# A hybrid Hyena, attention and expert layer: fewer transfers for attention's values, a merge that begins with the attention branch, and two banks for the first expert's tokens

## The chip, the cores and the metric

The kernel runs on one core of one Trainium2 chip. The metric is the device time of one execution in microseconds; a time is the median of several executions. The engines are TensorE (PE, with PEld for its weight loads), VectorE (DVE), ScalarE (ACT), GpSimd (POOL) and SyncE (SP). SP and POOL issue nearly all the transfers.

## What is computed

One layer over 1024 latent tokens (a grid of 16 rows by 64 columns) and 256 context tokens, width 1024, everything in float32:

```python
hx = modulate(rmsnorm(x), sh1, sc1); zx = hx @ w_in + b_in      # one combined projection
hy_x = hyena_mixer(zx[..., :COL_Q], ...)                        # two long convolutions
na_x = na_latent(q, k, v, kc, vc, rpb)                          # neighbourhood attention, 8 heads
a = hy_x @ w_branch_hy;  b = na_x @ w_branch_na                 # the merge
mix = (sigmoid(g_hy) * a + sigmoid(g_na) * b) @ w_out
x = x + g1 * mix
h = modulate(rmsnorm(x), sh2, sc2)
aff = softmax(h @ w_router); g, idx = top_k(aff.T, 128)         # 16 experts choose 128 tokens each
y_e = (silu(h[idx] @ wg) * (h[idx] @ wu)) @ wd                  # per expert
x = x + g2 * scatter_add(g_e * y_e);  out = rmsnorm(x) * final_g
```

Attention for a query uses keys and values in a window of 8 rows by 16 columns, and all 256 context tokens.

## The kernel before

The work is a row of blocks, one after the other: projection, attention (`attend`), Hyena (`hyena`), `merge`, `project_out`, `choose`, `experts`. In a block each engine has its own program and they wait for one another by semaphores; no engine begins the next block before all have ended this one. Each float32 product is made of three products of parts: an operand is split by ACT into a rounded high part (`*_hi`), by DVE into the rest (`*_lo = raw - hi`), and TensorE multiplies hi by hi, hi by lo and lo by hi.

**Values.** The last part of the projection computes the values, tile by tile of 128 tokens: TensorE fills a bank, DVE adds the bias into `v_stage` (L841), POOL stores the tile to `v_d` in DRAM (L392). Attention wants them laid out in `v_band`: a block holds four grid rows by a box of 32 columns, on 128 partitions. `load_values(sp, a, keep, kg)` loads, for the four grid rows of `kg`, four boxes `b`, in four transfers each, one for each grid row `r`. SP issues those of `kg` 0 to 2 at the end of the projection block, behind the stores of the normed tokens' parts to `hq_d` (L351), each `kg` behind a wait for two tiles stored (`stored`); then it waits for `kept`, and the block may end. Those of `kg` 3 it issues first in the attention block, behind the last tiles' stores; behind them come the tables and the heads (`load_table`, `load_head`). The first product of attention's probabilities and values waits for `v_in[0]` (`kg` 0 to 2), the fifth for `v_in[1]`. TensorE's steps in attention are: scores of step s, transposes of step s-2, product of step s-3.

**End of Hyena.** Hyena has four passes (p from 0 to 3) and the gates' projection (`gates(n)`, 32 of them, products L1399) is spread between them by the table `SHARE`. In the last pass DVE makes `products` and `transform` (L1512 to L1552), then raises `y_ready`; TensorE makes `outputs(3, i)` for i from 0 to 3 (L1382) and DVE `gated(3, i)` (L1564, L1572), which end the block with `y_t`. ACT's last works are the gates' sigmoids (L1454); SP stores each (L1275).

**Merge.** SP loads the first slices of the branch weights (`b_raw`), then attention's output `na_d` into `na_t`, then weights and gates (`g_d`). ACT and DVE split `y_t` (4 quarters), the weights' slice 0, then `na_t` (4 quarters). TensorE multiplies for output slice d=0: Hyena's branch for both token halves, then attention's; each branch of a half is 12 matmuls of 512 columns. DVE gates and adds. The loop over d from 1 to 7 follows.

**Experts.** The weights come in units of 1 MB (`raw`, 8 slots, 33 units for each expert, 528 in all); ACT splits a unit (L2251), DVE makes its low part (L2303), TensorE uses it in 12 matmuls (L2210 gate and up, L2200 down). Units 0 and 1 are the gate's of chunk 0 (unit 0 uses the tokens' rows k 0 to 3, unit 1 k 4 to 7), 2 and 3 the up's, 4 to 7 those of chunk 1. ACT and DVE take work in one written order:

```python
for g in range(N_ALL + N_U):
    if AHEAD <= g < N_ALL:
        split(g)
    for e, what, c in steps(g):
```

By that order DVE's `multiply` of chunk 0 (`moe_h`, L2324) stands behind `split(9)`, and ACT's `silu` behind `split(7)`. `split(g)` for g of 6 and more waits until unit g-6 is used. After unit 5 TensorE transposes this `h` (`turn_h(0, 0)`, L2181) and then goes to unit 6. At the start POOL gathers the first expert's tokens `xe`; TensorE transposes them in two halves (`turn_x`, L2173, four transposes each) in one bank `ps_x`; ACT copies the high part (L2244), DVE the low part (L2294). The second half's transposes wait for the first half's low part, and unit 0 waits for both. DVE makes the splits 0 to 2, three small works and only then the low parts.

Of the kernel before, what the change touches and what calls it, by code (L numbers as in the profile page):

```python
# [9 lines left out]
F32 = mybir.dt.float32  # L10
# [6 lines left out]
P = 128  # L17
# [865 lines left out]
def attend(nc, sems, a, keep):  # L883
# [3 lines left out]
    with ExitStack() as ctx:  # L887
# [55 lines left out]
        with nc.Block() as block:  # L943
# [23 lines left out]
            def _(pe):  # L967
# [206 lines left out]
def hyena(nc, sems, a, keep, y_t):  # L1174

    par, ident = keep["par"], keep["ident"]
    with ExitStack() as ctx:
# [25 lines left out]
        decay_in, gate_in, v2_in = keep["w_mod_in"][0:3]  # L1203
        LOADED = 16 * MOD_CHUNKS
# [48 lines left out]
        with nc.Block() as block:  # L1253

            @block.sync
            def _(sp):
# [178 lines left out]
            def _(act):  # L1435
# [20 lines left out]

                for p in range(-1, PASSES):
# [17 lines left out]
                    for n in AT_END[p]:  # L1475
                        gates(n)

            @block.vector
            def _(dve):
# [107 lines left out]
                for p in range(PASSES):  # L1587
                    q = p + 1
                    coming = iter(range(PH if q < PASSES else 0))

                    def decay_next():
                        for r in itertools.islice(coming, 1):
# [5 lines left out]
                    for r in coming:  # L1598
# [10 lines left out]

def merge(nc, sems, a, keep, y_t, m_t):  # L1610

    with ExitStack() as ctx:
        m = Maker(nc, ctx, "merge_")
        in_hi, in_lo = m.sb("in_hi", [P, 2, 4, T], F32R), m.sb("in_lo", [P, 2, 4, T], F32R)
        na_t = m.sb("na_t", [P, 4, T])
        b_raw = m.sb("b_raw", [P, 2, 2, 4, P])
        b_hi, b_lo = m.sb("b_hi", [P, 2, 2, 4, P], F32R), m.sb("b_lo", [P, 2, 2, 4, P], F32R)
        gate = m.sb("gate", [P, 2, 2, T])
        ps = m.psum("ps", [P, 4, 2, 512])


        w_in = [sems(f"branch_in{s}") for s in range(2)]
        g_in = [sems(f"gates_in{s}") for s in range(2)]
        na_in = sems("na_in")
        in_hi_ready, in_lo_ready, bh_ready, bl_ready, branched, merged = (
            sems(n) for n in ("in_hi_ready", "in_lo_ready", "bh_ready", "bl_ready", "branched", "merged"))

        with nc.Block() as block:

            @block.sync  # L1630
            def _(sp):
                w = [a[n].rearrange("(k p) (d c) -> d p k c", p=P, c=P) for n in ("w_branch_hy", "w_branch_na")]
                g = a["g_d"].rearrange("(b d p) t -> b d p t", b=2, p=P)
                wo = a["w_out"].rearrange("(k p) n -> p k n", p=P)
                for b in range(2):
                    sp.dma_start(b_raw[:, 0, b], w[b][0]).then_inc(w_in[0], 16)
                for k in range(4):
                    sp.dma_start(na_t[:, k], a["na_d"][k]).then_inc(na_in, 16)
# [14 lines left out]
            def _(pe):  # L1653
                pe.sem_inc(branched, 4)

                def branch(s, th, b, first=False):
                    for k in range(4):
                        if first:
                            pe.wait_ge(in_lo_ready, 4 * b + k + 1)
                        hi, lo = b_hi[:, s, b, k, :], b_lo[:, s, b, k, :]  # L1660
                        cols = slice(th * 512, (th + 1) * 512)
                        for x, (w, h) in enumerate(((hi, in_hi), (hi, in_lo), (lo, in_hi))):
                            mm = pe.matmul(ps[:, 2 * s + th, b, :], w, h[:, b, k, cols],
# [17 lines left out]
            def _(act):  # L1681
# [5 lines left out]
                for b, src in enumerate((y_t, na_t)):  # L1687
                    if b:
                        split(0, 0, 0)
                        act.wait_ge(na_in, 64)  # L1690
                    for k in range(4):
# [813 lines left out]
```

## Time and profile before

| | |
|---|---|
| median of three runs | 2703.47 us (2702.67 to 2703.78) |
| the profiled execution's own time | 2703.3 us |
| its span, first to last instruction | 2700.7 us |
| PE busy | 2545.6 us, 94% |
| DVE busy | 2121.3 us, 79% |
| ACT busy | 1469.9 us, 54% |
| mean granted TensorE clock | 0.973 |
| bytes moved | 794.93 MB, mean 294 GB/s |

The profile is one execution. A share of busy time is a mean over stages; what a stage is worth is read from its own stretch. The time outside the span is 2.6 us.

### The profile page before, as it was taken

How to read it: one execution, taken by the hardware profiler on the slowest of the kernel's cores; microseconds unless marked ns; L12 is line 12 of the kernel's file. 1: busy time of each engine (PE TensorE's matmuls, PEld its weight loads, DVE VectorE, ACT ScalarE, POOL GpSimd, SP SyncE). 2: the span in 40 equal slices, each digit the busy share in tenths (PEclk: the TensorE clock that was granted, in tenths of full speed). 3: DMA queues.
4: the chain of work that ended last, by engine and by line, in shares of the span. 5: the costliest groups of instructions: out<-in, count | busy, mean ns of one | idle time of the engine just before them, and what ended most of it. 6: DMA issues, size and time to landing. Idle time of an engine off the chain costs nothing.

```text
span 2700.7 us, 32209 instructions
## 1 busy us (share of the span) xinstructions
PE 2545.6 (94%) x12577; PEld 2121.3 (79%) x12577; DVE 2121.3 (79%) x1976; ACT 1469.9 (54%) x1249; POOL 149.3 (6%) x159
## 2 busy tenths in 40 slices
PE   6999979999999899389999999999999999999997
PEld 2777869878878778368888888888888888888885
DVE  5674247667879555688888888889888888888887
ACT  4522136531121222177777777777777777777774
POOL 0011000011111000000000000000000000000000
PEclk9999989999999999689999999999999999999998
DMA  7498774464566733399999999999999999999994
GB/s 272 161 314 306 248 228 111 135 200 140 162 200 197 236 104 131 155 339 362 386 390 373 374 392 381 363 383 394 370 373 392 380 366 383 389 375 367 392 382 171
DMA packets 198628, 794.93 MB, mean 294 GB/s; under 512 B 17935, under 2 KB 65399, under 8 KB 128528
## 3 DMA queue, kind: packets, MB, share of 16 engines
q1 hardware_dynamic: 168196, 704.75, 69.4%
q0 software_dynamic: 30128, 88.11, 10.6%
q8 instruction: 98, 1.61, 0.2%
q14 instruction: 48, 0.39, 0.0%
q10 hardware_dynamic: 158, 0.07, 0.0%
HBM read 723.38 MB, written 69.48 MB: 294 GB/s over the span
## 4 chain that ended last, share of the span: by engine, by line
PE 53%; ACT 2%; issue 2%; DVE 1%; DVEq 0%; ACTq 0%
PE moe_ps_gate L2210 18%; PE moe_ps_up L2210 16%; PE moe_ps_y L2200 16%; PE moe_ps_h L2181 2%; ACT moe_w_hi L2251 1%; PE moe_ps_x L2173 1%; DVE raw L2373 0%; ACT moe_xt_hi L2244 0%; DVE moe_w_lo L2303 0%; DVE moe_h L2324 0%; ACT moe_sl L2264 0%; DVE raw L2360 0%; PE moe_ps_gate L2234 0%; PE moe_ps_gate L2236 0%; PE moe_ps_up L2234 0%
## 5 line engine op out<-in xcount | busy, mean ns | idle before, releaser
L2303 DVE TENSOR_TENSOR moe_w_lo<-raw,moe_w_hi 128x2048 fp32r<-128x2048 f32 x528 | 1207.6, 2290 | 159.8 <-ACT moe_w_hi L2251 159.6
L2251 ACT ACTIVATE moe_w_hi<-raw 128x2048 fp32r<-128x2048 f32 x528 | 1011.0, 1919 | 379.2 <-PE moe_ps_gate L2210 128.4
L2210 PE MATMUL moe_ps_up<-moe_w_hi,moe_xt_hi 128*128 128x512 f32 (+1 forms) x768 | 292.4, 381 | 0.0
L2210 PE MATMUL moe_ps_gate<-moe_w_hi,moe_xt_hi 128*128 128x512 f32 (+1 forms) x768 | 289.1, 376 | 1.4 <-DVE moe_xt_lo L2294 1.4
L2210 PE MATMUL moe_ps_gate<-moe_w_hi,moe_xt_lo 128*128 128x512 f32 (+1 forms) x768 | 286.5, 373 | 0.0
L2210 PE MATMUL moe_ps_up<-moe_w_hi,moe_xt_lo 128*128 128x512 f32 (+1 forms) x768 | 286.4, 373 | 0.0
L2210 PE MATMUL moe_ps_gate<-moe_w_lo,moe_xt_hi 128*128 128x512 f32 (+1 forms) x768 | 286.1, 373 | 0.0
L2210 PE MATMUL moe_ps_up<-moe_w_lo,moe_xt_hi 128*128 128x512 f32 (+1 forms) x768 | 285.9, 372 | 0.0
L2200 PE MATMUL moe_ps_y<-moe_w_hi,moe_ht_hi 128*128 128x512 f32 x704 | 218.5, 392 | 0.0
L2200 PE MATMUL moe_ps_y<-moe_w_hi,moe_ht_lo 128*128 128x512 f32 x704 | 217.0, 389 | 0.0
L2200 PE MATMUL moe_ps_y<-moe_w_lo,moe_ht_hi 128*128 128x512 f32 x704 | 217.0, 389 | 0.0
L1399 PE MATMUL hyena_ps_g<-hyena_h_parts,hyena_g_parts 128*128 128x512 f32 x768 | 182.5, 395 | 2.0 <-DMA hyena_h_parts<-hq_d 1.9
L1399 PEld LDWEIGHTS hyena_ps_g<-hyena_h_parts,hyena_g_parts 128*128 128x128 f32 x768 | 144.0, 188 | 33.3 <-issue 1.9
L2210 PEld LDWEIGHTS moe_ps_gate<-moe_w_hi,moe_xt_hi 128*128 128x128 f32 x768 | 145.2, 189 | 26.4 <-DVE moe_xt_lo L2294 1.8
L2210 PEld LDWEIGHTS moe_ps_gate<-moe_w_hi,moe_xt_lo 128*128 128x128 f32 x768 | 145.1, 189 | 25.6
L2210 PEld LDWEIGHTS moe_ps_gate<-moe_w_lo,moe_xt_hi 128*128 128x128 f32 x768 | 145.3, 189 | 24.8
L2210 PEld LDWEIGHTS moe_ps_up<-moe_w_hi,moe_xt_lo 128*128 128x128 f32 x768 | 144.5, 188 | 25.6
L2210 PEld LDWEIGHTS moe_ps_up<-moe_w_lo,moe_xt_hi 128*128 128x128 f32 x768 | 144.8, 189 | 23.7
L2210 PEld LDWEIGHTS moe_ps_up<-moe_w_hi,moe_xt_hi 128*128 128x128 f32 x768 | 144.7, 188 | 23.3
L2200 PEld LDWEIGHTS moe_ps_y<-moe_w_lo,moe_ht_hi 128*128 128x128 f32 x704 | 132.2, 188 | 27.8
L2200 PEld LDWEIGHTS moe_ps_y<-moe_w_hi,moe_ht_lo 128*128 128x128 f32 x704 | 132.2, 188 | 27.7
L1512 DVE TENSOR_TENSOR hyena_spec<-hyena_spec 128x1024 f32<-128x1024 f32 (+2 forms) x120 | 139.4, 1217 | 16.1 <-ACT hyena_spec L1447 15.8
(278 smaller groups left out, 3707.1 us busy)
## 6 DMA issues: line engine op xcount, KB each, us to landing
raw<-in_w_moe SPq DMA_DIRECT2D x528, 1024.0 KB, 7.2
hyena_g_parts<-gw_d POOLq DMA_DIRECT2D x64, 512.0 KB, 4.7
proj_w_mod<-in_w_mod SPq DMA_DIRECT2D x32, 512.0 KB, 7.3
gw_d<-proj_g_parts POOLq DMA_DIRECT2D x16, 1024.0 KB, 7.4
w_in<-in_w_in SPq DMA_DIRECT2D x12, 1024.0 KB, 7.6
attn_table<-in_na_table SPq DMA_DIRECT2D x16, 576.0 KB, 5.6
norm_w_mod<-in_w_mod SPq DMA_DIRECT2D x16, 512.0 KB, 7.1
proj_g_raw<-in_w_in SPq DMA_DIRECT2D x16, 512.0 KB, 9.5
```

The costliest lines, as they stand in the source:

```text
L1399: mm = pe.matmul(ps_g[:, n % 2, :], g_parts[:, g % G_SLOTS, w, k % G_K, :], h_parts[:, h, k, :], start=(k == 0 and y == 0), stop=(k == KD ...
L1512: dt.inc(dve.tensor_tensor(out, in0, in1, op))
L2173: mm = pe.transpose(ps_x[:, k * P:(k + 1) * P], xe[:, at:at + P], ident[:])
L2181: mm = pe.transpose(ps_h[:, b * P:(b + 1) * P], h[:, c % 2, b * P:(b + 1) * P], ident[:])
L2200: mm = pe.matmul(ps_y[:, n * 512:(n + 1) * 512], hp, wp[:, r, n * 512:(n + 1) * 512], start=(first and x == 0), stop=(last and x == 2))
L2210: mm = pe.matmul(ps, hp[:, e % 2, k, :], wp[:, r, :], start=(k == 0 and x == 0), stop=(k == KD - 1 and x == 2))
L2251: act.activation(w_hi[:, g % PARTS], raw[:, g % RAW], ACT.Copy).then_inc(hi_ready, 1)
L2303: dve.tensor_tensor(w_lo[:, g % PARTS], raw[:, g % RAW], w_hi[:, g % PARTS].bitcast(F32), ALU.subtract).then_inc(lo_ready, 1)
```

## The change

Three parts. (A) `load_values` issues one transfer for each box instead of one for each box and grid row: its source has three dimensions (4 grid rows, 32 columns, 512 numbers of 4 bytes), its target all 128 partitions. The counts waited for shrink to match. (B) The merge's tiles are placed before Hyena; SP, ACT and DVE load and split slice 0 of the branch weights and the first quarter of attention's output inside Hyena's last pass (`na_raw` has three slots; the fourth quarter is loaded once the first is split), ACT makes the high parts of the other quarters at the end of the Hyena block, DVE their low parts first in the merge block; TensorE takes attention's branch first. (C) In the expert block, 36 transposes of the identity stand ahead of the first `turn_x`; the second half of expert 0 goes to the bank `ps_h`; unit 0 waits for the first half only, unit 1 for the second; DVE makes the two low parts after split 1.

```diff
-def load_values(sp, a, keep, kg):
+def load_values(eng, a, keep, kg):
     for b in range(4):
-        for r in range(4):
-            first = (4 * kg + r) * GRID_W + BAND_AT[b]
-            sp.dma_start(keep["v_band"][BAND * r:BAND * (r + 1), v_block(kg, b), 0:HEADS * HD],
-                         a["v_d"][first:first + BAND]).then_inc(keep["v_in"][kg // 3], 16)
+        first = 4 * kg * GRID_W + BAND_AT[b]
+        rows = bass.AP(a["v_d"].tensor, first * HEADS * HD, [[GRID_W * HEADS * HD, 4], [HEADS * HD, BAND], [1, HEADS * HD]])
+        eng.dma_start(keep["v_band"][:, v_block(kg, b), 0:HEADS * HD], rows).then_inc(keep["v_in"][kg // 3], 16)
...
-                        pe.wait_ge(v_in[g], 16 * 48 if g == 0 else 16 * 16)
+                        pe.wait_ge(v_in[g], 16 * 12 if g == 0 else 16 * 4)
...
+                def load_na(k):
+                    s = k % NA_SLOTS
+                    if k >= NA_SLOTS:
+                        sp.wait_ge(na_lo_ready, k - NA_SLOTS + 1)
+                    sp.dma_start(coming["na_raw"][:, s], a["na_d"][k]).then_inc(na_in, 16)
...
+                        if p == PASSES - 1 and r == 1:
+                            sp.wait_ge(tap_used, PH * PASSES)
+                            sp.wait_ge(a_done, a_at["seg", p, PH - 1] + 1)
+                            for b, w in enumerate(branch_sources(a)):
+                                sp.dma_start(coming["b_raw"][:, 0, b], w[0]).then_inc(branch_in[0], 16)
+                            for k in range(NA_SLOTS):
+                                load_na(k)
...
+                load_na(NA_SLOTS)
                 sp.wait_ge(g_kept, 16 * N_G)
...
+                    if p == PASSES - 1:
+                        act.wait_ge(branch_in[0], 32)
+                        act.activation(coming["b_hi"][:, 0], coming["b_raw"][:, 0], ACT.Copy).then_inc(bh_ready, 1)
+                        act.wait_ge(out_done, NB * p)
+                        high_na(0)
...
+                for k in range(1, 4):
+                    high_na(k)
...
                     dve.sem_inc(y_ready, 1)
-                    for r in coming:
+                    if p == PASSES - 1:
+                        dve.wait_ge(bh_ready, 1)
+                        dve.tensor_tensor(coming["b_lo"][:, 0], coming["b_raw"][:, 0], coming["b_hi"][:, 0].bitcast(F32),
+                                          ALU.subtract).then_inc(bl_ready, 1)
+                        low_na(dve, coming, 0)
+                    for r in decays_left:
...
+def low_na(dve, at, k):
+    dve.wait_ge(at["in_hi_ready"], k + 1)
+    dve.tensor_tensor(at["lo"][1][:, k], at["na_raw"][:, k % NA_SLOTS], at["hi"][1][:, k].bitcast(F32), ALU.subtract
+                      ).then_inc(at["in_lo_ready"], 1)
...
                 pe.wait_ge(bl_ready, 3)
-                branch(0, 0, 0, first=True)
-                branch(0, 1, 0)
+                branch(0, 0, 1, first=True)
+                branch(0, 1, 1)
                 for th in range(2):
-                    branch(0, th, 1, first=not th).then_inc(branched, 1)
+                    branch(0, th, 0, first=not th).then_inc(branched, 1)
...
+                for k in range(1, 4):
+                    low_na(dve, at, k)
+                for k in range(4):
+                    dve.wait_ge(in_hi_ready, 4 + k + 1)
+                    dve.tensor_tensor(in_lo[0][:, k, :], y_t[:, k, :], in_hi[0][:, k, :].bitcast(F32),
+                                      ALU.subtract).then_inc(in_lo_ready, 1)
...
+        WARM = 36
...
+        def x_turned(e, half):
+
+            return ps_h if (e, half) == (0, 1) else ps_x
...
+                for n in range(WARM):
+                    pe.transpose(ps_x[:, n % 4 * P:(n % 4 + 1) * P], ident[:], ident[:])
                 turn_x(0, 0)
                 turn_x(0, 1)
                 for e in range(E_N):
-                    pe.wait_ge(x_parts, 2 * e + 2)
+                    if e:
+                        pe.wait_ge(x_parts, 2 * e + 2)
                     for u in range(N_U):
+                        if e == 0 and u < 2:
+                            pe.wait_ge(x_parts, u + 1)
...
-                for g in range(AHEAD):
+                split(0)
+                split(1)
+                for half in range(2):
+                    low_x(0, half)
+                for g in range(2, AHEAD):
                     split(g)
```

## Rows read from the trace of the kernel before

**Rows 1.** The chain that ended last, in order of time: start, duration, what

```profile
1182.76 5.51 PE moe_ps_up L2210 x24
...
1276.95 5.49 PE moe_ps_up L2210 x24
```

**Rows 2.** Timeline, 355 to 400 us: start, duration, engine, line, what, [idle before, releaser]

```profile
360.09 0.54 POOL L392 DMA_DIRECT2D v_d<-attn_v_stage  x1 [4.95 <-DVE attn_v_stage L841]
...
373.26 0.66 PE L990 MATMUL attn_ps_s<-attn_k_hi,attn_q_two 128*128 128x384 f32 x1 [14.20 <-PEq L266]
...
381.92 1.82 PE L1022 MATMUL attn_ps_o<-v_band,attn_prob_t 128*128 128x128 f32 x10
```

**Rows 3.** Timeline of SP's queue, 325 to 400 us, then 370 to 374 us

```profile
332.89 3.78 SPq L351 DMA_DIRECT2D hq_d<-h_lo  x1
336.78 43.62 SPq L163 DMA_DIRECT2D v_band<-v_d  x64
...
369.87 4.50 SPq L163 DMA_DIRECT2D v_band<-v_d  x9
```

**Rows 4.** Lines 163, 392, 351 (landing), 1275: issue ns min/median/max, landing

```profile
L163 SPq DMA_DIRECT2D v_band<-v_d x64: 312/422/8769, 336.8 to 380.0; - x64
DMA to landing us min/median/max: 1.8/1.9/15.1
...
DMA to landing us min/median/max: 2.7/5.8/8.9
...
DMA to landing us min/median/max: 18.5/22.2/24.5
...
L1275 SPq DMA_DIRECT2D g_d<-hyena_g_out x6: 319/320/320, 849.8 to 876.6; - x6
```

**Rows 5.** Timeline of all engines, 856 to 912 us

```profile
877.39 7.77 PE L1382 MATMUL hyena_ps_out<-idft,hyena_spec 128*128 128x128 f32 x64 [1.74 <-DVEq L1597]
879.48 0.87 DVE L1564 SCALAR_TENSOR_TENSOR y_t<-y_t,par,hyena_ps_out 128x256 f32<-128x256 f32 x2 [2.20 <-PE hyena_ps_out L1382]
...
886.16 0.76 DVE L1572 TENSOR_TENSOR y_t<-y_t,hyena_gate 128x256 f32<-128x256 f32 x2
...
887.22 3.90 ACT L1692 ACTIVATE merge_in_hi<-y_t 128x1024 fp32r<-128x1024 f32 x4 [10.68 <-PEq L1253]
...
888.31 4.63 DVE L1726 TENSOR_TENSOR merge_in_lo<-y_t,merge_in_hi 128x1024 fp32r<-128x1024 f32 x4 [1.39 <-ACT merge_in_hi L1692]
...
892.86 1.22 DVE L1705 TENSOR_TENSOR merge_b_lo<-merge_b_raw,merge_b_hi 128x1024 fp32r<-128x1024 f32 x1
...
894.13 0.79 PE L1663 MATMUL merge_ps<-merge_in_hi,merge_b_hi 128*128 128x512 f32 x1 [8.97 <-DVE merge_b_lo L1705]
...
907.46 1.29 DVE L1716 TENSOR_TENSOR merge_gate<-merge_ps,merge_gate 128x512 f32<-128x512 f32 x2 [0.47 <-PE merge_ps L1663]
```

**Rows 6.** Windows: us; busy PE, PEld, DVE, ACT, POOL; clock, DMA share, GB/s

```profile
373.00:383.00 10.00, 8.11 (x32) 7.58 (x33) 8.03 (x14) 6.81 (x9) 0.00 (x0) 0.50 0.51 134
...
1163.00:1168.00 5.00, 4.92 (x12) 3.86 (x13) 3.82 (x3) 4.70 (x3) 0.00 (x0) 0.50 0.80 298
```

**Rows 7.** Timeline of all engines, 1143 to 1186 us

```profile
1152.41 6.70 DVE L2303 TENSOR_TENSOR moe_w_lo<-raw,moe_w_hi 128x2048 fp32r<-128x2048 f32 x3 [2.22 <-ACT moe_w_hi L2251]
...
1156.48 1.12 PE L2173 MATMUL moe_ps_x<-identity,moe_xe 128*128 128x128 f32 x4 [7.33 <-DMA moe_xe<-h_d,idx_col]
1157.63 0.60 ACT L2244 ACTIVATE moe_xt_hi<-moe_ps_x 128x512 fp32r<-128x512 f32 x1 [1.66 <-PE moe_ps_x L2173]
...
1159.80 0.69 DVE L2294 TENSOR_TENSOR moe_xt_lo<-moe_ps_x,moe_xt_hi 128x512 fp32r<-128x512 f32 x1 [0.21 <-DVE moe_chosen L2312]
...
1163.08 0.80 PE L2210 MATMUL moe_ps_gate<-moe_w_hi,moe_xt_hi 128*128 128x512 f32 x1 [1.41 <-DVE moe_xt_lo L2294]
...
1164.20 11.33 DVE L2303 TENSOR_TENSOR moe_w_lo<-raw,moe_w_hi 128x2048 fp32r<-128x2048 f32 x5 [1.18 <-ACT moe_w_hi L2251]
...
1181.36 0.68 DVE L2324 TENSOR_TENSOR moe_h<-moe_sl,moe_ps_up 128x512 f32<-128x512 f32 x1
```

More of the change, by code:

```diff
@@ L1203, in hyena @@
         decay_in, gate_in, v2_in = keep["w_mod_in"][0:3]
+        coming = keep["merge"]
+        branch_in, na_in, na_hi_ready, na_lo_ready, bh_ready, bl_ready = (
+            coming[n] for n in ("w_in", "na_in", "in_hi_ready", "in_lo_ready", "bh_ready", "bl_ready"))
         LOADED = 16 * MOD_CHUNKS
@@ L1607, in _, with merge_places, branch_sources @@
                         transform(U_LEAF[q], U_SPEC[q], nothing)
+NA_SLOTS = 3
+def merge_places(nc, sems):
+    with ExitStack() as ctx:
+        m = Maker(nc, ctx, "merge_")
+        at = {"b_raw": m.sb("b_raw", [P, 2, 2, 4, P]),
+              "b_hi": m.sb("b_hi", [P, 2, 2, 4, P], F32R), "b_lo": m.sb("b_lo", [P, 2, 2, 4, P], F32R)}
+        m.sb("room", [P, PH * 2 * P])
+        at["na_raw"] = m.sb("na_raw", [P, NA_SLOTS, T])
+        hi, lo = [None, None], [None, None]
+        hi[0], hi[1] = m.sb("y_hi", [P, 4, T], F32R), m.sb("na_hi", [P, 4, T], F32R)
+        at["gate"] = m.sb("gate", [P, 2, 2, T])
+        lo[0], lo[1] = m.sb("y_lo", [P, 4, T], F32R), m.sb("na_lo", [P, 4, T], F32R)
+        at["hi"], at["lo"] = hi, lo
+    at["w_in"] = [sems(f"branch_in{s}") for s in range(2)]
+    for n in ("na_in", "in_hi_ready", "in_lo_ready", "bh_ready", "bl_ready"):
+        at[n] = sems(n)
+    return at
+def low_na(dve, at, k):
+    dve.wait_ge(at["in_hi_ready"], k + 1)
+    dve.tensor_tensor(at["lo"][1][:, k], at["na_raw"][:, k % NA_SLOTS], at["hi"][1][:, k].bitcast(F32), ALU.subtract
+                      ).then_inc(at["in_lo_ready"], 1)
+def branch_sources(a):
+    return [a[n].rearrange("(k p) (d c) -> d p k c", p=P, c=P) for n in ("w_branch_hy", "w_branch_na")]
 def merge(nc, sems, a, keep, y_t, m_t):
@@ L1613, in merge @@
         m = Maker(nc, ctx, "merge_")
[L1614 to L1618, printed above, removed]
+        at = keep["merge"]
+        b_raw, b_hi, b_lo, gate, in_hi, in_lo = (at[n] for n in ("b_raw", "b_hi", "b_lo", "gate", "hi", "lo"))
         ps = m.psum("ps", [P, 4, 2, 512])
-        w_in = [sems(f"branch_in{s}") for s in range(2)]
+        w_in, in_hi_ready, in_lo_ready, bh_ready, bl_ready = (
+            at[n] for n in ("w_in", "in_hi_ready", "in_lo_ready", "bh_ready", "bl_ready"))
         g_in = [sems(f"gates_in{s}") for s in range(2)]
-        na_in = sems("na_in")
-        in_hi_ready, in_lo_ready, bh_ready, bl_ready, branched, merged = (
-            sems(n) for n in ("in_hi_ready", "in_lo_ready", "bh_ready", "bl_ready", "branched", "merged"))
+        branched, merged = (sems(n) for n in ("branched", "merged"))
         with nc.Block() as block:
@@ L1685, in split @@
                     act.activation(b_hi[:, s], b_raw[:, s], ACT.Copy).then_inc(bh_ready, 1)
[L1687 to L1691, printed above, removed]
-                        act.activation(in_hi[:, b, k, :], src[:, k, :], ACT.Copy).then_inc(in_hi_ready, 1)
+                for k in range(4):
+                    act.activation(in_hi[0][:, k, :], y_t[:, k, :], ACT.Copy).then_inc(in_hi_ready, 1)
                 with act.Fori(0, KD // 2 - 1) as i:
@@ L2166, in turn_x @@
                 def turn_x(e, half):
-                    if half or e:
+                    if e:
                         pe.wait_ge(x_parts, 2 * e + half)
@@ L2172, in turn_x @@
                         at = (4 * half + k) * P
-                        mm = pe.transpose(ps_x[:, k * P:(k + 1) * P], xe[:, at:at + P], ident[:])
+                        mm = pe.transpose(x_turned(e, half)[:, k * P:(k + 1) * P], xe[:, at:at + P], ident[:])
                     mm.then_inc(turned_x, 1)
@@ L2254, in _ @@
                     split(g)
-                high_x(0, 0)
-                high_x(0, 1)
+                for half in range(2):
+                    high_x(0, half)
                 for g in range(N_ALL + N_U):
@@ L2304, in split @@
                                       ALU.subtract).then_inc(lo_ready, 1)
-                for g in range(AHEAD):
+                split(0)
+                split(1)
+                for half in range(2):
+                    low_x(0, half)
+                for g in range(2, AHEAD):
                     split(g)
@@ L2417, in program @@
                 y_t = Maker(nc, mixer).sb("y_t", [P, 4, T])
+                keep["merge"] = merge_places(nc, sems)
                 n = Maker(nc, convolving)
```

35 lines of the change are left out of this document (15 added, 20 removed).

## The prediction, made before the changed kernel was seen

> **What bounds the kernel now.** I read the chain that ended last first. From unit 6 of the first expert on it is TensorE alone: the same matmuls of the up part come 94.19 us apart [rows 1], and so on to the last expert. So nothing of this change lasts beyond the first expert, and what moves unit 6 moves the end by as much. Ahead of the experts the blocks follow one another with a meeting of all engines between them, so a block that ends sooner brings everything forward. I then looked, with the timeline, for TensorE's long idle times ahead of unit 6 in the places that the diff touches. There are three: 14.20 us before attention's first matmul [rows 2], 8.97 us before the merge's first [rows 5], and the wait before the first expert's first matmul, which begins at 1163.08 though the tokens had come by 1156.48 [rows 7]. The clock column of the windows says what they also cost: granted 0.50 (1.2 GHz) in the first 10 us of attention and in the first 5 us of the experts [rows 6].
>
> **Part A, attention's values.** TensorE and DVE are done with the projection by 359.8, and POOL's last work in it, the issue of the last value tile's store, ends at 360.09 + 0.54 = 360.63 [rows 2]. ACT has long been idle. What ends the block is SP: nine issues take 4.50 us, 0.50 each, and the 64 of them end at 380.40 [rows 3]. Sixteen belong to the next block, so the 48th ended about 16 x 0.46 = 7.4 us sooner, at 373.0, and attention starts at 373.1 to 373.3 [rows 2]. The change leaves 12 issues in this block. What does one of four times the size take? From below, 0.32 us: the store of the gates' bank is also 256 KB, 128 rows of 2 KB [rows 4]. From above, four times the small one, 4 x 0.46 = 1.8 us, if the issue goes by rows. I take 0.5, near the row with the same shape. The first issue is held up for 8.77 us behind the four stores to `hq_d`, of which the last was issued at 332.89 [rows 3] and lands 22.2 us later in the median, at 355 [rows 4]. Even if the first group of four boxes is held until then, the other 8 issues take 4 us: 359. The third group also waits for a tile whose store is two tiles of 5.49 us ahead of the last, at 349.1 [rows 2], and lands 5.8 us later (at most 8.9): 355 to 358, and 4 issues more, 357 to 360. The wait for `kept` is over by about 355. So SP ends at 357 to 360, before POOL's 360.63; the meeting costs about 0.3 (886.92 to 887.20 at the end of Hyena [rows 5]), and attention starts at 360.9 instead of 373.2: 12.3 us gained. What is late next? The first product needs the three groups' data; it stood 8.7 us after the block's start [rows 2], which gives 369.6, and the last of those transfers, issued by 360, has until then (landing 1.9 in the median for the small ones [rows 4]). The fourth group waits for the last tile's store, 360.6 + 5.8 = 366.4, then 4 x 0.5 and its landing: about 372, against the fifth product at about 379. The tables and heads behind it on SP's queue come 9 us or more earlier than before. The clock: TensorE now idles 2 us instead of 14, but its first ten microseconds are filled only 8.11 of 10 at the low clock [rows 6] and DVE has its own long works there; between nothing and 1.5 us more; I take 0.4. Part A: -12.7.
>
> **Part B, the merge.** Inside Hyena it adds, on SP, two transfers of 256 KB and three of 512 KB behind the second of the six gate stores of this stretch (849.8 to 876.6, so 5.4 us apart in the mean [rows 4]). At 0.5 us an issue [rows 3] they take 2.5 us, less than the distance to the next store. Their two waits are for Hyena's tap and segment work of the pass before, over by then. Their 2 MB compete with the gates' weights; TensorE waits 1.74 us at the end of this pass for DVE [rows 5], which covers that much delay, and I charge nothing. ACT gets two copies of about 1 us (its quarters cost 3.90 / 4) ahead of its last sigmoid, which ended 10.68 us before 887.22, at 876.5 [rows 5]; nobody but its own store waits for it, which has 10 us: covered. DVE gets 1.22 + 1.16 us behind `y_ready` (quarters cost 4.63 / 4) and had 2.20 us idle there [rows 5]: 0.2 to 0.4 late, I take +0.3. At the end SP's fourth quarter is issued at 880.2, and if it lands as a value tile of half its size does at most, 5.8 us later [rows 4], ACT's copy ends at 887: about the block's own end, so the block ends at 887.2 + 0.3.
>
> In the merge, DVE needs 3 x 1.16 for attention's quarters 1 to 3 (until 891.0), then 4 x 1.16 for `y_t` (until 895.7). ACT's `y_t` copies take 3.90 [rows 5] and are ahead of it. TensorE starts at 887.6 on quarter 0. At the low clock 12 matmuls take 5 us [rows 6], at the full one 24 take 5.5 [rows 1]. If it starts low, attention's first half fills 887.8 to 892.9; with the clock up then (as at the experts' start, where it stayed low for 5 us of matmuls [rows 6]), three groups of 12 at 2.73 follow: 901.1; Hyena's last quarter at 895.7 is in time for its use after 895.7. If it stays high throughout: DVE's 891.0 + 0.7, then 2.7 three times: 899.9. Before, the 48 matmuls began at 894.13 and were done by 907.0 (DVE waits 0.47 us and gates from 907.46 [rows 5]). Gain 5.9 or 7.1, less 0.3 already in the start of the first; I take 5.9. Slice 1's weights are issued at 887.7 and are wanted as low part at 901: 13 us for a landing, a copy of 1 and a difference of 1.22 [rows 5]. Part B: -5.9, between -4.5 and -7.
>
> **Part C, the first expert.** This is the part where the obvious sum misleads. TensorE's side: tokens at 1156.48, four transposes 1.12, ACT 0.60, DVE 0.69 [rows 7]; with the new order unit 0 can start at 1156.5 + 1.15 + 0.65 + 0.7 = 1159.0 instead of 1163.08, and if the extra transposes have raised the clock, it saves the 2.3 us by which the first 12 matmuls (5.0 us [rows 6]) exceed 2.7. That reads as 4.1 + 2.3 = 6.4 us. But after unit 5 TensorE needs `h` of chunk 0, and DVE's multiply stands behind its splits 2 to 9. It ended at 1181.36 + 0.68 = 1182.04 with DVE nearly full from 1164.20 on: five splits in 11.33, 2.26 each [rows 7]. In the changed order DVE has splits 0 and 1 until 1152.41 + 4.5 = 1156.9, waits for ACT until 1158.3, then 2 x 0.69, split 2 (2.26), its small works 0.5, splits 3 to 9 (7 x 2.26 = 15.8) and the multiply 0.68: 1158.3 + 1.4 + 2.3 + 0.5 + 15.8 + 0.7 = 1179.0. ACT's splits and the units that they wait for run ahead of that. TensorE would be through unit 5 by 1159.0 + 6 x 2.72 = 1175.3 and then wait 3.7 us, a new wait in place of the old. Unit 6 gains 1182.0 - 1179.0 = 3.0 us, clock or no clock. After it DVE is again in time: splits 10 and 11 and the low part of `h` end at 1184.3, unit 8 needs them at 1185.1.
>
> The 36 transposes are no gain by this sum, only a risk: four at the low clock take 1.12 [rows 7], 0.23 each, so 36 take up to 8.3 us from the block's start, until 1158.8 (ACT's first split, of which DVE's at 1152.41 waits, puts the start at 1150.5 [rows 7]); if the clock rises after 5 us and the rest run at about half that, they end at 1157.1. The first means the tokens' transposes start 2.3 us late and DVE's row of work with them: gain 0.8. The second 0.6 late: 2.5. I take 2.5, as dense TensorE work has raised the clock within some 5 us at this place before [rows 6], and keep 0.8 as a case of its own.
>
> The Trainium skill, page "TensorE: Matmul & The Clock Gate", section "Part 4: PE-mode transpose", says that transposes in that mode do not bring on the full clock, as they don't count as TensorE activity in the same way. No row here has transposes alone for so long, so none agrees or disagrees. By it part C would be -0.8 instead of -2.5.
>
> **Sum.** -12.7 - 5.9 - 2.5 = -21.1 us. The profiled execution, 2700.7 of span and 2.6 outside it, becomes 2679.6 and 2.6, 2682.2; its 2703.3 is 0.2 under the median, so 2682.4.
>
> **The rivals.** (1) *The issue goes by rows, not by transfer*, or the 12 large ones are held up behind `hq_d` as long as the 48 were. For it: the first issue was held up for 8.77 us. Against: the 256 KB store issued in 0.32 [rows 4]. Part A gives 0 to 4 instead of 12.7: 2691 to 2695. (2) *TensorE's own sum holds in part C*: DVE's splits would have to take 1.8 us instead of 2.26, as nine works stand ahead of the multiply; against it, those five in 11.33 us [rows 7]. Part C -6.4, 2678.5. (3) *The transposes stay slow*: all 36 run at the pace of the four, end at 1158.8, 2.3 us after the tokens have come, and hold back the tokens' transposes and DVE: part C -0.8, 2684.1. (4) *Part B does nothing*, as the fourth quarter lands late or the gates' weights are delayed beyond the 1.74 us: 2688.3. (5) *Slower.* The transfers over four boxes land so late that attention stands at its first product, which waits for all 12. They are 3 MB; while the small ones moved, the core's traffic was 134 GB/s [rows 6]. The start of the first product is 369.6 if they are in time, and part A's 12.7 and the others' 8.4 would have to be lost, so the case decides once they land after 369.6 + 21.1 = 390.7; at 396, 5 us slower, 2709. That is 3 MB in 36 us from 360, under 90 GB/s; against it stand the 298 GB/s of the experts' start [rows 6].
>
> **How the numbers follow.** The forecast (2679.5 to 2686 by its own bounds): 0.44. Rival 3: 0.30. Rival 1: 0.08. Rival 2 and other larger gains, the clock in attention among them: 0.08. Rival 4: 0.05. Rival 5: 0.03. A result near no change, A, B and C all losing what they gave: 0.02. 0.2% is 5.4 us, about what a measurement of this kernel tells from no change. Faster 0.95, same 0.02, slower 0.03. The parts' bounds are A -11 to -14, B -4.5 to -7, C -0.8 to -6.4: -16.3 to -27.4 if all fell together, of which the far end is unlikely; I give 2677.5 to 2689.5, which leaves out rivals 1, 5 and the worse half of 4.
>
> **What the changed profile would show.** Attention's first matmul 2 to 3 us after the projection's last, with SP no longer last (wrong if SP's issues run past 361). The merge's first matmul within 0.7 us of the block's start, its first gating by DVE about 13 us after it. In the experts: the 36 transposes end before or after the tokens come, with the clock column at 0.5 or 1.0; unit 0 4 us earlier against the block's start; and a new wait of 2 to 4 us of `turn_h(0, 0)` for DVE's `moe_h`. If that wait is missing and unit 6 is 6 us earlier, step C is wrong. The prediction is wrong as a whole if the start of attention doesn't move.

## The result, and the profile after

The changed kernel takes 2711.96 us (median of 7 runs, 2710.43 to 2715.95) where the kernel before took 2702.75 beside it (7 runs, 2700.76 to 2703.78): a ratio of 1.0039, 95% interval 1.0030 to 1.0048. It is 9.2 us slower; 21 us faster was forecast. The profiled execution took 2712.3 us.

Read part by part, the loss lies in one place. First attention's start, in the timeline of the changed kernel, SyncE's queue and then the rows of TensorE, ScalarE and VectorE that waited. These rows answer to [rows 2, 3]:

```profile
335.53 47.61 SPq L163 DMA_DIRECT2D v_band<-v_d  x16
383.19 5.49 SPq L156 DMA_DIRECT2D attn_table<-in_na_table  x2
388.78 3.24 SPq L148 DMA_DIRECT2D attn_q_raw<-qk_d  x1
396.63 2.21 SPq L156 DMA_DIRECT2D attn_table<-in_na_table  x2
398.94 3.04 SPq L148 DMA_DIRECT2D attn_q_raw<-qk_d  x1
...
373.96 0.66 PE L989 MATMUL attn_ps_s<-attn_k_hi,attn_q_two 128*128 128x384 f32 x1 [15.95 <-PEq L265]
384.65 1.97 PE L1021 MATMUL attn_ps_o<-v_band,attn_prob_t 128*128 128x128 f32 x10 [2.21 <-DMA v_band<-v_d]
401.96 2.50 PE L1021 MATMUL attn_ps_o<-v_band,attn_prob_t 128*128 128x128 f32 x10 [6.42 <-DMA v_band<-v_d]
413.17 1.30 PE L973 MATMUL attn_ps_t<-identity,attn_prob 128*128 128x128 f32 x5 [3.52 <-ACT attn_prob_t L1054]
...
406.92 0.82 DVE L1103 CUSTOM_DVE_ANT_0 attn_score<-attn_ps_s,attn_table 128x640 f32<-128x640 f32 x1 [1.93 <-DMA attn_table<-in_na_table]
411.38 1.06 ACT L853 ACTIVATE attn_q_two<-attn_q_raw 128x1024 fp32r<-128x1024 f32 x1 [2.58 <-DMA attn_k_raw<-qk_d]
```

Sixteen issues end at 383.14, where 64 ended at 380.40 [rows 3]. Attention starts at 373.96, 16.3 us behind the projection's last matmul (357.62), where it was 14.6. Then TensorE stands twice for the values (2.21 and 6.42 us), and behind them on SyncE's queue the tables and heads are late as well: VectorE waits 1.93 us for a table, ScalarE 2.58 for a head, TensorE 3.52 for ScalarE. From its first matmul to Hyena's first matmul, attention takes 180.8 us instead of 164.7.

The duration of the 16 issues (view of one line: count, shortest/median/longest in ns, first and last start), and the windows of the changed kernel (columns as in [rows 6]):

```profile
L163 SPq DMA_DIRECT2D v_band<-v_d x16: 1780/2548/6878, 335.5 to 380.8; - x16
...
365.00:370.00 5.00, 0.00 (x0) 0.00 (x0) 0.00 (x0) 0.00 (x0) 0.00 (x0) 0.50 0.26 98
370.00:374.00 4.00, 0.04 (x1) 0.07 (x1) 0.00 (x0) 0.23 (x1) 0.00 (x0) 0.50 0.26 98
390.00:400.00 10.00, 5.54 (x47) 5.33 (x44) 4.90 (x16) 4.93 (x7) 0.00 (x0) 0.95 1.04 199
```

An issue takes 2.55 us, not 0.5. The two last columns say why to look at the transfer and not at the queue: while nothing but these transfers moves, the DMA engines are busy a steady 0.26 of the time, at 98 GB/s. That share is a mean over 16 engines, so 0.26 is what four of the sixteen give if they are at work all the time. The trace's single packets bear it out: from 365 to 373 us four packets are in flight in 84% of the instants, and never fewer. Before, the small transfers moved 144 GB/s from 365 to 370 us.

The merge and the first expert gained nearly what was forecast. Merge, VectorE's splits of attention's quarters, and the gating that answers to the one at 907.46 in [rows 5]:

```profile
905.72 0.47 PE L1719 MATMUL merge_ps<-merge_na_hi,merge_b_hi 128*128 128x512 f32 x1 [2.38 <-DVEq L1753]
905.60 3.50 DVE L1667 TENSOR_TENSOR merge_na_lo<-merge_na_raw,merge_na_hi 128x1024 fp32r<-128x1024 f32 x3 [0.50 <-PEq L1255]
919.29 1.29 DVE L1768 TENSOR_TENSOR merge_gate<-merge_ps,merge_gate 128x512 f32<-128x512 f32 x2 [0.47 <-PE merge_ps L1719]
```

The merge's block starts at 905.4, so this gating comes 13.9 us into the merge, where it was 20.3: 6.4 us gained. From Hyena's first matmul to that start it is 350.6 us instead of 349.2. Experts, TensorE and VectorE, the rows that answer to [rows 7]:

```profile
1162.56 6.25 PE L2273 MATMUL moe_ps_x<-identity 128*128 128x128 f32 x36 [1.35 <-PEq L2034]
1168.96 0.65 PE L2229 MATMUL moe_ps_x<-identity,moe_xe 128*128 128x128 f32 x4 [0.16 <-DMA moe_xe<-h_d,idx_col]
1174.55 15.51 DVE L2366 TENSOR_TENSOR moe_w_lo<-raw,moe_w_hi 128x2048 fp32r<-128x2048 f32 x7
1189.96 0.68 DVE L2389 TENSOR_TENSOR moe_h<-moe_sl,moe_ps_up 128x512 f32<-128x512 f32 x1
1190.70 1.05 PE L2239 MATMUL moe_ps_h<-identity,moe_h 128*128 128x128 f32 x4 [3.06 <-DVE moe_h L2389]
```

The new wait of `turn_h(0, 0)` for VectorE's multiply is there, 3.06 us long (3.7 forecast). It has a price that the forecast left out. The granted clock is still 1.00 while TensorE waits, and 0.50 once it works again, so the 24 matmuls of units 6 and 7 take 6.69 us where they took 5.51 before ([rows 1], 1182.76). The windows are read as in [rows 6], the last row is from the chain that ended last:

```profile
1188.00:1190.00 2.00, 0.00 (x0) 0.00 (x0) 2.00 (x2) 1.65 (x1) 0.00 (x0) 1.00 0.99 418
1191.00:1194.00 3.00, 3.00 (x10) 2.52 (x9) 3.00 (x2) 1.09 (x2) 0.00 (x0) 0.50 1.00 418
...
1191.76 6.69 PE moe_ps_up L2268 x24
```

### The profile page after: what moved, and what is told of

It reads as the page before. It is cut to its first block, busy times and chain, and to the rows that moved or that the text cites. A ratio compares the mean times of both kernels' runs of the same rounds, so it can differ in the third digit from the quotient of the medians.

```text
span 2710.6 us, 32235 instructions
## 1 busy us (share of the span) xinstructions
PE 2554.4 (94%) x12613; PEld 2129.3 (79%) x12613; DVE 2121.2 (78%) x1976; ACT 1469.6 (54%) x1249; POOL 149.1 (6%) x159
## 4 chain that ended last, share of the span: by engine, by line
PE 52%; issue 2%; ACT 2%; DVE 1%; DMA 0%; DVEq 0%; ACTq 0%; POOLq 0%
PE moe_ps_gate L2268 18%; PE moe_ps_y L2258 16%; PE moe_ps_up L2268 16%; PE moe_ps_h L2239 2%; ACT moe_w_hi L2314 1%; PE moe_ps_x L2229 1%; DVE moe_w_lo L2366 0%; DVE raw L2438 0%; ACT moe_xt_hi L2307 0%; DVE moe_h L2389 0%; ACT moe_sl L2327 0%; DMA moe_xe<-h_d,idx_col 0%; DVE raw L2425 0%; PE moe_ps_gate L2297 0%; PE moe_ps_gate L2299 0%
## 5 line engine op out<-in xcount | busy, mean ns | idle before, releaser
L2258 PEld LDWEIGHTS moe_ps_y<-moe_w_lo,moe_ht_hi 128*128 128x128 f32 x704 | 132.2, 188 | 27.8
L2258 PEld LDWEIGHTS moe_ps_y<-moe_w_hi,moe_ht_lo 128*128 128x128 f32 x704 | 132.2, 188 | 27.8
L1540 DVE TENSOR_TENSOR hyena_spec<-hyena_spec 128x1024 f32<-128x1024 f32 (+2 forms) x120 | 139.6, 1219 | 16.1 <-ACT hyena_spec L1463 15.8
```

The lines of the kernel that those rows point to most:

```text
L1540: dt.inc(dve.tensor_tensor(out, in0, in1, op))
L2258: mm = pe.matmul(ps_y[:, n * 512:(n + 1) * 512], hp, wp[:, r, n * 512:(n + 1) * 512], start=(first and x == 0), stop=(last and x == 2))
```

## The experiments

Theory 1: a transfer whose source pattern has an outermost dimension of 4 is carried by 4 of the 16 DMA engines; it is slow, holds back the issue of the next, and all that stands behind it. Theory 2: an issue costs by its rows or bytes. Theory 3: the stores of `hq_d` in front hold everything up. Each kernel is compared with the kernel before on the same chip: bc_only, rows128, by_row and two_rows with 2701.87 us (12 runs), a_only, last_stores, two_queues and no_warm with 2702.82 (11 runs), early_multiply and last_stores_again with 2701.96 (11 runs). The table gives, for the profiled execution of each kernel, how many us behind the projection's last matmul attention's first one starts, and how many us pass from there to Hyena's first matmul.

| kernel | median, us | start of attention | attention |
|---|---|---|---|
| before | 2702 to 2703 | 14.6 | 164.7 |
| after | 2711.96 | 16.3 | 180.8 |
| bc_only | 2692.77 | 13.3 | 165.0 |
| a_only | 2722.01 | 16.4 | 180.5 |
| rows128 | 2687.27 | 8.4 | 164.6 |
| by_row | 2690.95 | 10.6 | 164.6 |
| two_rows | 2753.68 (one run) | 48.0 | 192.0 |
| last_stores | 2682.28 | 3.8 | 164.5 |
| two_queues | 2683.64 | 3.3 | 164.6 |

### The parts by themselves: bc_only and a_only

bc_only leaves `load_values` and its counts as they were before; a_only changes `load_values` and its counts and nothing else.

> Parts B and C alone; the values are loaded as before. If part A is the whole loss, and B and C are worth what the two traces show (the merge 5.0 us net, the first expert 2.4), this runs at 2702.8 - 7.4 = 2695.4 us, and the merge's first matmul stands 0.5 us behind its block's start. If B or C carries a loss of its own, it is at 2700 or more.

> Part A alone (16 transfers of 256 KB over four grid rows), the merge and the first expert as in the kernel before. If the parts add up, after less what B and C give (9.1 us measured in bc_only, on another chip): 2702 + 9.2 + 9.1 = about 2720; traffic of 98 GB/s from 365 to 380. If A did harm only together with B or C (their loads behind the same queue), it is below 2712.

bc_only: ratio 0.9968 (0.9958 to 0.9979), 9.1 us faster. a_only: 1.0078 (1.0062 to 1.0095), 19.2 us slower. Their sum, +10.1, is the changed kernel's +9.2 within their intervals. So B and C give about what they should (8.4 forecast), and all of the loss, and more, is part A's. In a_only's trace it sits where it did in the changed kernel: 1.8 us in attention's start and 15.8 in attention.

### The same bytes from rows that follow one another: rows128

```diff
-        rows = bass.AP(a["v_d"].tensor, first * HEADS * HD, [[GRID_W * HEADS * HD, 4], [HEADS * HD, BAND], [1, HEADS * HD]])
-        eng.dma_start(keep["v_band"][:, v_block(kg, b), 0:HEADS * HD], rows).then_inc(keep["v_in"][kg // 3], 16)
+        eng.dma_start(keep["v_band"][:, v_block(kg, b), 0:HEADS * HD], a["v_d"][first:first + P]
+                      ).then_inc(keep["v_in"][kg // 3], 16)
```

> The changed kernel, but each of the 16 transfers reads 128 rows of v_d that follow one another, instead of four rows of the grid by 32 columns: the same 256 KB, 128 pieces of 2 KB, onto the same 128 partitions. It leaves out the choice of the right rows, so attention multiplies by wrong values; all else is as before. Theory 1 (a source whose outermost dimension is 4 is carried by 4 of the 16 DMA engines, and the slow transfers hold back their own issue and all behind them): the issues fall from 2.55 to 0.3-0.5 us each, attention's first matmul comes at about 360.5, the traffic there is 2 to 3 times 98 GB/s, and the time is about 2683. Theory 2 (an issue costs by its bytes or rows, whatever the pattern): 2.5 us each as in the changed kernel, 2712. Theory 3 (the stores of hq_d in front hold all up): 2712 too, with a first issue held for about 7 us and the others slow.

Measured 2687.27 us, ratio 0.9954 (0.9938 to 0.9971), 24.7 us under the changed kernel with the same 16 transfers of 256 KB onto the same 128 partitions. The line, and a window in which the fourth group moves:

```profile
L162 SPq DMA_DIRECT2D v_band<-v_d x16: 319/446/8560, 335.8 to 366.9; - x16
...
365.00:370.00 5.00, 3.19 (x12) 2.93 (x13) 2.80 (x8) 2.88 (x3) 0.00 (x0) 0.50 0.57 196
374.00:380.00 6.00, 5.93 (x48) 5.76 (x48) 5.57 (x14) 4.56 (x7) 0.00 (x0) 0.95 1.00 171
```

The issue fell from 2.55 to 0.45 us in the median with rows and bytes unchanged: theory 2 is out. Theory 3 is out too, as the `hq_d` stores are the same; what they do is hold up the first issue, for 8.56 us, as before the change. But the time is 4 us over theory 1's 2683, and attention's first matmul is at 365.76, not 360.5. That is taken up below.

### Two rows of the grid in a transfer: two_rows

```diff
-        first = 4 * kg * GRID_W + BAND_AT[b]
-        rows = bass.AP(a["v_d"].tensor, first * HEADS * HD, [[GRID_W * HEADS * HD, 4], [HEADS * HD, BAND], [1, HEADS * HD]])
+        for r in range(0, 4, 2):
+            first = (4 * kg + r) * GRID_W + BAND_AT[b]
+            rows = bass.AP(a["v_d"].tensor, first * HEADS * HD, [[GRID_W * HEADS * HD, 2], [HEADS * HD, BAND], [1, HEADS * HD]])
...
```

> The changed kernel with the values in 32 transfers of 128 KB, each of two grid rows by 32 columns (outermost dimension 2 instead of 4); nothing of the computation changes. Theory 1: 2 of the 16 engines, so about 49 GB/s and a DMA share of 0.13 in 365 to 374; the 3 MB that the first product waits for need 64 us instead of 32, and the time is 2735 to 2775. Theory 2 (by bytes or rows): 32 issues of 1.27, 2708 to 2714. If the number of transfers alone counts: about 2707, between the kernel before and the changed one.

One run, 2753.68 us, 52 us over the kernel before. Half the bytes in each transfer, and yet the issue takes the same 2.57 us; the rate and the share are half of the changed kernel's:

```profile
L164 SPq DMA_DIRECT2D v_band<-v_d x32: 1756/2567/6472, 335.8 to 423.7; - x32
...
365.00:370.00 5.00, 0.00 (x0) 0.00 (x0) 0.00 (x0) 0.00 (x0) 0.00 (x0) 0.50 0.13 49
...
405.77 0.66 PE L991 MATMUL attn_ps_s<-attn_k_hi,attn_q_two 128*128 128x384 f32 x1 [47.61 <-PEq L267]
```

49 GB/s and 0.13 for an outermost dimension of 2, 98 and 0.26 for one of 4: 24.5 GB/s for each engine that takes part, if it is 2 and 4 of them. In two_rows two packets are in flight in 91% of the instants from 365 to 373 us, and never fewer. The number of rows, the bytes and the number of transfers all fail to give that.

### Columns outermost: by_row

```diff
...
+    for r in range(4):
+        for x in range(0, 4, 2):
+            first = ((4 * kg + r) * GRID_W + BAND_AT[x]) * HEADS * HD
+            boxes = bass.AP(a["v_d"].tensor, first, [[HEADS * HD, BAND], [8 * HEADS * HD, 2], [1, HEADS * HD]])
+            eng.dma_start(keep["v_band"][BAND * r:BAND * (r + 1), v_block(kg, x):v_block(kg, x) + 2, 0:HEADS * HD], boxes
+                          ).then_inc(keep["v_in"][kg // 3], 16)
```

The waits count 24 and 8 transfers.

> The changed kernel with the values in 32 transfers of 128 KB: each is one grid row, two boxes that stand 8 columns apart, the 32 columns being the outermost dimension of source and target; nothing of the computation changes. Theory 1: all 16 engines carry each, an issue takes about 0.46 us as the small ones did, the 24 of the projection block end by about 355 + 4, attention's first matmul comes at 360.5 to 362, time 2682 to 2686. Theory 2 (by bytes): 1.27 us an issue, 16 MB... the same sum as in the changed kernel, 2708 to 2712. Theory 3: as theory 2.

Measured 2690.95 us, ratio 0.9963 (0.9949 to 0.9976): the issue takes 0.43 us, and the kernel is 21 us under the changed one. It has the same number of transfers and the same bytes in each as two_rows, whose issues took 2.57 us, and unlike rows128 it doesn't read 128 rows that follow one another; so neither the number and size of the transfers nor rows that follow one another make the difference. But the kernel is only 2 us under bc_only and 5 over the forecast; the start of attention again lags.

### Who ends the projection block: last_stores and two_queues

In rows128 SyncE was through with its issues early. Its waits, and the timeline around the block's end:

```profile
SPq L265 <- PEq L265: 8.0, 1, 8.0
...
358.75 0.54 POOL L391 DMA_DIRECT2D v_d<-attn_v_stage  x1 [4.96 <-DVE attn_v_stage L840]
365.76 0.66 PE L989 MATMUL attn_ps_s<-attn_k_hi,attn_q_two 128*128 128x384 f32 x1 [8.04 <-PEq L265]
```

SyncE stood 8.0 us at the block's end, VectorE 7.35. The last thing that any engine did was GpSimd's issue of the last value tile's store, ending at 359.29; attention's first matmul came 6.5 us later, and such a store lands in 5.8 us in the median [rows 4]. In by_row the issue ended at 361.80 and attention came at 370.48. The traces have the landing of this very store: 4.4 us after its start in rows128, 6.6 in by_row, and 7.4 in no_warm, which comes below. In all three attention's first matmul stands 2.6 us behind that landing. Theory D: the block ends only when the stores that GpSimd issued have landed. last_stores gives the last two to ScalarE:

```diff
-                for t in range(TT):
+                for t in range(TT - 2):
                     pool.wait_ge(evacuated, V_AT + 2 + t + 1)
...
+                for t in range(TT - 2, TT):
+                    act.wait_ge(evacuated, V_AT + 2 + t + 1)
+                    act.dma_start(a["v_d"][t * P:(t + 1) * P], v_stage[:, t % 2]).then_inc(keep["late_v"], 16)
...
-                    sp.wait_ge(stored[x], 16 * (SEG_V[0] + 4))
+                    sp.wait_ge(stored[x], 16 * (SEG_V[0] + 3))
+                sp.wait_ge(keep["late_v"], 32)
```

> by_row with one thing more: the stores of the last two value tiles are issued by ACT, idle there for 47 us, instead of POOL. In by_row and rows128 attention's first matmul stood 10.2 and 8.0 us behind the projection's last although SP was through with its issues 7 to 8 us earlier. Theory D (a block does not end before the stores that POOL issued have landed; the last is issued at 358.8 to 361.3 and takes 5.9 us and more): with POOL's last store now tile 5's, the block ends when SP's 24 issues do, at 359 to 363; attention starts 1 to 4 us behind the projection's last matmul instead of 10.2, and the time is 2682 to 2685. Rival E (the wait is SP's own queue or the loads' landing): no change, 2690 to 2691.

> last_stores, and the 8 transfers of kg 2 are issued by ACT too, in its own queue. If SP's 24 issues still bound last_stores, attention starts within 2.5 us of the projection's last matmul, 0 to 3 us sooner than in last_stores: 2680 to 2684. If not, the same as last_stores. If attention then stands at its first product, that many us are lost again.

last_stores: 2682.28 us, ratio 0.9924 (0.9912 to 0.9937), 20.5 us faster than before, 8.7 under by_row. Its timeline, and SyncE's waits:

```profile
354.28 5.88 ACTq L660 DMA_DIRECT2D v_d<-attn_v_stage  x2
362.44 0.66 PE L995 MATMUL attn_ps_s<-attn_k_hi,attn_q_two 128*128 128x384 f32 x1 [3.42 <-PEq L267]
...
SPq L953 <- DMA v_d<-attn_v_stage: 5.5, 1, 5.5
SPq L267 <- PEq L267: 0.2, 1, 0.2
```

Attention starts 3.8 us behind the projection's last matmul instead of 10.6. The landing still takes its time: SyncE now waits 5.5 us for it, but inside the attention block (L953), ahead of the fourth group, where nobody needs it yet. The last store was issued at 359.78 and landed 7 us or more later, well after attention's start at 362.44. Rival E falls. What ends the block is again SyncE (0.2 us of waiting). two_queues took 8 of its issues away; attention started 3.3 us behind instead of 3.8 (its forecast for this case was 2.5 or less), and the time is the same within the intervals (0.9932, 0.9919 to 0.9945). There is half a microsecond left in this place.

### Part C: no_warm and early_multiply

no_warm is by_row with `WARM = 0`.

> by_row without the 36 transposes ahead of the first expert's tokens. My theory of part C (VectorE's row of splits sets the multiply, and the transposes buy nothing): the multiply of chunk 0 begins 27.4 us behind TensorE's old first transpose, or at most 0.5 earlier or later, TensorE's wait for it shrinks from 3.1 us to about 1, time 2690 to 2691.5. Rival (the raised clock is what gains): the multiply is unchanged but unit 6 starts 2 us or more later, 2693.

One run, 2688.5 us, inside by_row's spread (2687.8 to 2694.3) and under both forecasts. From VectorE's last step of `choose` to the multiply it is 27.8 us, as in by_row (27.9), and the wait for it is now 0.78. Behind it stand units 6 and 7 from the chain that ended last, first those of no_warm, then those of by_row:

```profile
1167.51 0.68 DVE L2391 TENSOR_TENSOR moe_h<-moe_sl,moe_ps_up 128x512 f32<-128x512 f32 x1
1168.24 0.66 PE L2241 MATMUL moe_ps_h<-identity,moe_h 128*128 128x128 f32 x4 [0.78 <-DVE moe_h L2391]
...
1168.90 5.51 PE moe_ps_up L2270 x24
...
1168.27 7.72 PE moe_ps_up L2270 x24
```

The 36 transposes let TensorE arrive earlier and wait longer, and in the longer wait the granted clock falls: by_row has 0.50 from 1167 to 1172, no_warm 1.00 from 1168 to 1172. So the transposes don't merely gain nothing here, they cost. From the experts' start (ScalarE's first split) to unit 8, just behind units 6 and 7, it is 37.8 us in the kernel before, 35.4 to 37.7 in the eight traces that have the transposes and the wait of 3 us, and 34.3 in no_warm.

early_multiply is last_stores with VectorE's order changed for splits 9 and 11 of the first expert:

```diff
-                    if AHEAD <= g < N_ALL:
+                    if AHEAD <= g < N_ALL and g not in (9, 11):
                         split(g)
                     for e, what, c in steps(g):
...
+                    if g in (9, 11):
+                        split(g)
```

> last_stores with VectorE's order changed for the first expert only: the multiply of chunk 0 stands ahead of split 9 instead of behind it, the low part of h ahead of split 11. My theory of part C (the multiply waits for VectorE's row of splits): it begins 2.26 us sooner after the experts' start, TensorE's wait of 3.0 us for it shrinks to about 0.8, and unit 6 comes 2.2 us sooner: about 2 us below last_stores on the same chip. Rival (TensorE's wait is for ScalarE's silu or for its own units): the multiply waits where it now stands, no change.

> last_stores once more, for the comparison with early_multiply on one chip: 0.9924 of the kernel before, 2682 us.

early_multiply: 2678.96 us, ratio 0.9913 (0.9899 to 0.9926); last_stores beside it 2680.55, 0.9923 (0.9908 to 0.9937). These times alone don't tell the two apart. The traces do; early_multiply's two rows, then last_stores_again's:

```profile
1134.46 6.04 PE L2279 MATMUL moe_ps_x<-identity 128*128 128x128 f32 x36 [1.35 <-PEq L2040]
1160.38 0.66 PE L2245 MATMUL moe_ps_h<-identity,moe_h 128*128 128x128 f32 x4 [0.82 <-DVE moe_h L2395]
```

```profile
1129.93 5.63 PE L2279 MATMUL moe_ps_x<-identity 128*128 128x128 f32 x36 [1.34 <-PEq L2040]
1157.97 1.11 PE L2245 MATMUL moe_ps_h<-identity,moe_h 128*128 128x128 f32 x4 [3.07 <-DVE moe_h L2395]
```

The wait goes from 3.07 to 0.82 us and `turn_h` comes 25.9 us behind the first transpose instead of 28.0. `turn_h` also takes 0.66 instead of 1.11: after the longer wait TensorE was granted 0.50 of its clock (windows, 1158 to 1161), after the shorter one 1.00 (1160.4 to 1163). Units 6 and 7 then take 5.48 us instead of 7.72. From the experts' start to unit 8 it is 32.1 us instead of 36.9, a gain of 4.8 in this pair of traces, of which 2.1 is the earlier multiply and the rest the clock; about 2 was forecast. VectorE's row of splits is what this place waits for. The clock follows the length of the wait and not the transposes as such, since early_multiply has all 36 of them.

## Why the prediction was wrong, step by step

**Part A, the cost of an issue: the step that failed.** I priced the transfer by its size and target: "I take 0.5, near the row with the same shape". That row, the gates' store of 256 KB [rows 4], has 128 rows that follow one another; rows128 confirms its price (0.45 us). What the forecast left out is the pattern of the source, four grid rows outermost. It costs 2.55 us, five times as much, and the rate with it. Part A's -12.7 became +1.8 in attention's start and +16.1 within attention: 17.8, against 19.2 by the medians of a_only. The Trainium skill, page "DMA: Bandwidth & Descriptors", section "Why a DMA increments its semaphore by 16 and not by 1", states it: the number of engines is the largest one up to 16 that divides the outermost dimension (the first that isn't 1) of both sides. For 4 and 128 that is 4; the trace agrees, with a share of 0.26, and two_rows with 0.13. I had not weighed that rule.

**Rival 5 was close, and its price was right.** It said that the transfers over four boxes land so late that attention stands at its first product, below 90 GB/s, 2709 us. Measured: 98 GB/s and 2712. I gave it 0.03 because of 298 GB/s at the experts' start, a rate of transfers of another pattern. Its place was only half right: of the 16.1 us that attention takes longer, 8.6 are waits for the values; 3.5 are TensorE's wait for ScalarE, whose head came late on the same queue, and behind these waits the granted clock is lower too: 0.82 from 384 to 402 us and 0.76 from 402 to 415, where the kernel before has 1.00 from 395 to 415.

**Part A, what is late next: a second miss, hidden by the first.** "SP ends at 357 to 360, before POOL's 360.63; the meeting costs about 0.3." In rows128 SyncE was done in time, and attention started at 365.76. I counted GpSimd as done with its issue; the block waited on for the landing of its last store. So even with a price of 0.45 for the issue part A would have gained 6.2 us (14.6 to 8.4) and not 12.3. That a landing is what was waited for rests on two things: on last_stores, where only the last two stores (and SyncE's wait for them) moved to another queue, and on the constant 2.6 us between the landing and attention's start in rows128, by_row and no_warm. What passes in these 2.6 us no trace shows.

**Part B** was forecast at -5.9 and gave -5.0: 6.4 in the merge, less 1.4 in Hyena, where I had charged 0.3. There the new loads stand between two gate stores; the store issued behind them took until about 887.3 to land, and ScalarE waited for it:

```profile
873.78 1.67 SPq L1283 DMA_DIRECT2D merge_na_raw<-na_d  x3
877.99 0.32 SPq L1277 DMA_DIRECT2D g_d<-hyena_g_out  x1
887.39 0.69 ACT L1470 ACTIVATE hyena_g_out<-hyena_ps_g,par 128x512 f32<-128x512 f32 x1 [9.43 <-DMA g_d<-hyena_g_out]
```

"I charge nothing" for the 2 MB may be the error, but the size isn't shown. No run took these loads away by themselves, and Hyena takes 348.6 to 351.1 us in the ten traces with part B (the lowest in by_row), 349.2 and 349.6 in the two without it.

**Part C** was forecast at -2.5 and gave -2.2, in part by luck. The experts' start is 12.1 us later than before (1162.54 against 1150.47), and the span's end 9.9 (2710.6 against 2700.7). The step that unit 0's early start would be eaten by a wait for VectorE held, 3.06 us for 3.7. But "clock or no clock" did not hold: against the experts' start the multiply came 3.5 us earlier than before, and `turn_h` and units 6 and 7, at the fallen clock, then lost 1.6 of it. In other traces with the same part C they lost more: from the experts' start to unit 8 the gain was 0.8 us in by_row and 0.1 in two_queues. The forecast said that the transposes "are no gain by this sum, only a risk" and looked for the risk in the tokens' delay; it lay in the longer wait. Rival 2, TensorE's own sum, is out. Rival 3, with a chance of 0.30, is out as well: the transposes ended before they could hold back the tokens.

**The sum.** With -5.0 and -2.2 from B and C and +17.8 from A it is +10.6; the projection ended 1.1 us earlier in this execution, which leaves 9.5, against 9.9 between the spans and 9.2 between the medians. The chance of 0.95 for a faster kernel treated part A as a sum of known rows, while it hung on one price that no row showed.

## What to carry to other kernels

Before a transfer is made larger, read the outermost dimension of both its sides: fewer issues are no gain if only 4 of 16 DMA engines carry them, and a slow transfer delays all that stands behind it on its queue. Give the outermost place to a dimension that 16 divides, even if that needs twice the transfers. A block isn't over when its last store has been issued; if the store belongs to GpSimd, count its landing, or let an idle engine's queue issue it. And before TensorE is made to arrive earlier, look at what it will wait for: a new wait of 3 us brought the granted clock down, and the work behind it took 0.9 to 2.3 us longer.

## What the runs showed of the hardware

- DMA rate went with the outermost dimension of the source: 2 gave 49 GB/s, 4 gave 98, and an issue was held back for 2.55 us in both cases, for 128 KB as for 256 KB.
- Where the last store of the projection block was GpSimd's and SyncE was through, the next block's first matmul came 6.5, 8.7 and 9.4 us behind the end of that issue (rows128, by_row, no_warm), each time 2.6 us behind the landing. With ScalarE issuing the last two stores it did not wait for their landing.
- After a wait of 3.02 to 3.07 us TensorE was granted 0.50 of its clock (1.2 GHz), and its next 24 matmuls took 6.4 to 7.8 us (eight traces). After waits of 0.78 and 0.82 us, and in the two kernels without this wait, they took 5.5.
- Transposes alone raised TensorE's clock. In the changed kernel, the 36 of them, by windows:

```profile
1163.00:1167.00 4.00, 4.00 (x21) 4.00 (x20) 2.52 (x2) 4.00 (x3) 1.03 (x1) 0.51 0.75 244
1167.50:1168.80 1.30, 1.30 (x12) 1.07 (x10) 1.30 (x1) 0.56 (x1) 0.00 (x0) 1.00 0.72 180
```

TensorE did nothing else there, and the granted clock went from 0.51 to 1.00 (1.2 to 2.4 GHz). The Trainium skill, page "TensorE: Matmul & The Clock Gate", section "Part 4: PE-mode transpose", says that they don't bring the full clock; this trace, with float32 transposes, disagrees. It gained nothing here, since VectorE sets the pace, and it made the wait longer in which the clock fell again.
